# First layer of a two-layer encoder: another order of loads, norms, low halves and roots, four PSUM banks for the first tiles

## The reference, cut to what matters

```python
x = layer_norm(x, ln0_g, ln0_b)
for i in range(2):
    h = x @ w_in[i]                                  # 1024 -> 1536 columns
    qa, ka, va, qb, kb, vb = split(h)                # 512 | 128 | 128 | 512 | 128 | 128
    oa = softmax(rope2d(rms(qa)) @ rope2d(rms(ka)).T) @ va      # all keys
    ob = window_softmax_with_sink(rope1d(qb) @ rope1d(kb).T) @ vb
    mix = concat(rms(oa), rms(ob)) @ w_out[i]
    x = layer_norm(ALPHA * x + mix)
    gate = sigmoid(x @ w_ple_gate[i] + b)
    x = layer_norm(ALPHA * x + conv_glu(x) + gate * (p[i] @ w_ple[i]))
```

## Time and profile before

| | us |
|---|---|
| median of three runs | 1205.07 |
| the profiled execution | 1204.98 |
| its span (first to last instruction) | 1203.0 |
| TensorE busy | 1186.2 (99%) |
| VectorE, ScalarE, GpSimd busy | 524.5, 483.5, 585.3 |
| first matmul of the products | 15.97 |
| first scores | 70.25 |
| last matmul | 1195.08 |

### The profile page before, as it was taken

The page is one execution under the profiler, slowest core; times in us unless marked ns, Lnnn a source line. Parts: engine busy times, 40 slices in busy tenths (PEclk is TensorE's granted clock), DMA queues, the critical chain, the costliest instruction groups (busy, mean ns, idle before and its releaser), DMA issues.

```text
span 1203.0 us, 16482 instructions
## 1 busy us (share of the span) xinstructions
PE 1186.2 (99%) x5784; PEld 971.0 (81%) x5784; DVE 524.5 (44%) x1094; ACT 483.5 (40%) x890; POOL 585.3 (49%) x338
## 2 busy tenths in 40 slices
PE   7999999999999999999999999999999999999997
PEld 6787778888888888888888777788888888888886
DVE  7777857522121234211587788374221122431107
ACT  3457763244343333323144777433443343332310
POOL 6565754455444444343254756634554443434330
PEclk9999999999999999999999999999999999999999
DMA  6321213344333332223132202333433333322301
GB/s 223 87 71 54 89 53 106 122 125 138 97 95 87 105 106 88 88 92 104 54 80 79 73 34 71 140 105 88 140 106 103 99 93 96 97 74 102 105 35 70
DMA packets 121753, 113.45 MB, mean 94 GB/s; under 512 B 6752, under 2 KB 97888, under 8 KB 121696
## 3 DMA queue, kind: packets, MB, share of 16 engines
q1 hardware_dynamic: 121696, 112.71, 30.1%
HBM read 110.60 MB, written 2.10 MB: 94 GB/s over the span
## 4 chain that ended last, share of the span: by engine, by line
PE 95%; DVE 1%; POOL 1%; DVEq 1%; DMA 1%; issue 0%; SPq 0%
PE ps L1238 29%; PE ps L1240 28%; PE ps L1239 28%; PE ps L1404 3%; PE ps L1390 3%; PE ps L1378 1%; PE ps L1380 1%; PE ps L1248 1%; PE ps L1361 1%; POOL w_lo L544 1%; DMA x<-in_x_prompt_dram 1%; POOL ln_r L540 0%; DVEq L886 0%; DVEq L932 0%; PE ps L1415 0%
## 5 line engine op out<-in xcount | busy, mean ns | idle before, releaser
L534 POOL TENSOR_TENSOR w_lo<-raw,w_hi 128x1024 fp32r<-128x1024 f32 x188 | 453.1, 2412 | 404.6 <-ACT w_hi L645 404.5
L1238 PE MATMUL ps<-xt_hi,w_hi 128*128 128x512 f32 x704 | 273.9, 389 | 0.0
L1239 PE MATMUL ps<-xt_lo,w_hi 128*128 128x512 f32 x704 | 273.9, 389 | 0.0
L1240 PE MATMUL ps<-xt_hi,w_lo 128*128 128x512 f32 x704 | 273.9, 389 | 0.0
L645 ACT ACTIVATE w_hi<-raw 128x1024 fp32r<-128x1024 f32 x188 | 197.8, 1055 | 132.2 <-PE ps L1240 61.4
L1238 PE MATMUL ps<-w_hi,stat 128*128 128x512 f32 x480 | 187.8, 391 | 0.0
L1239 PE MATMUL ps<-w_lo,stat 128*128 128x512 f32 x480 | 187.1, 390 | 0.0
L1240 PE MATMUL ps<-w_hi,stat 128*128 128x512 f32 x480 | 187.1, 390 | 0.0
L1238 PEld LDWEIGHTS ps<-xt_hi,w_hi 128*128 128x128 f32 x704 | 132.2, 188 | 27.5
L1239 PEld LDWEIGHTS ps<-xt_lo,w_hi 128*128 128x128 f32 x704 | 132.2, 188 | 27.4
L1240 PEld LDWEIGHTS ps<-xt_hi,w_lo 128*128 128x128 f32 x704 | 132.2, 188 | 27.3
(11 more groups left out here) (123 smaller groups left out, 1323.7 us busy)
## 6 DMA issues: line engine op xcount, KB each, us to landing
raw<-in_w_up_dram SPq DMA_DIRECT2D x88, 512.0 KB, 3.8
raw<-in_w_down_dram SPq DMA_DIRECT2D x44, 512.0 KB, 3.2
raw<-in_w_in_dram SPq DMA_DIRECT2D x22, 512.0 KB, 3.7
raw<-in_w_out_dram SPq DMA_DIRECT2D x16, 512.0 KB, 3.3
raw<-in_w_ple_gate_dram SPq DMA_DIRECT2D x16, 512.0 KB, 3.3
scratch<-in_ln_g_dram SPq DMA_DIRECT2D x5, 512.0 KB, 4.1
scratch<-in_ln_b_dram SPq DMA_DIRECT2D x5, 512.0 KB, 6.0
raw<-in_w_ple_dram SPq DMA_DIRECT2D x4, 512.0 KB, 3.3
```

What stands on the lines that cost most here:

```text
L534: pool.tensor_tensor(w_lo[:, n, :], raw[:, n % RAW, :], w_hi[:, n, :].bitcast(F32), ALU.subtract).then_inc(w_split.sem, 1)
L1238: pe.matmul(out, a[0], b[0], start=first, stop=False)
L1239: pe.matmul(out, a[0], b[1], start=False, stop=False)
L1240: return pe.matmul(out, a[1], b[0], start=False, stop=last)
```

## The change

In the first layer alone, and before it:

- **Loads.** SyncE's order becomes tile 0 of x, slot 0, gain, shift, slot 1, tile 1, slot 2, tile 2, slot 3, tile 3. Before it was tile 0, gain, shift, tile 1, slots 0, 1, 2, tile 2, slot 3, tile 3.
- **GpSimd.** Root 0, low halves 0, 1, root 1, low halves 2, 3, root 2, low halves 4, 5, root 3, low halves 6, 7; then the roots of the rotations of c = 0 without low halves between them. c = 1 is as before.
- **VectorE.** The statistics of tile t + 1 and then `norm_lo(t)` follow the scaling of tile t. `norm_lo(3)` now stands before `gain_tables`, so both it and the tables stand before `rotate(0, 0)`. `qkt_lo` of n - 2 precedes `rotate` n (before: `qkt_lo` of n - 1 followed it).
- **TensorE.** The first product starts before tile 1 is transposed, in a new form, `first_quarter`: hi by hi, then the products with `xt_lo`, then those with `w_lo`, each group with its own wait. Tile 1 is transposed after the third quarter; `norm_in` 2 and 3 stand in the middle of products 1 and 2. Turned tiles 0 to 5 are transposed behind product 3, in the middle of 4, in the middle of and behind 5, behind 6, and in the middle of 7 (before: in the middle of 2, behind 2, 3, 4, 5, 6). `keep_warm` is 8, 4 and 3 rounds (before 8 and 9), the last inside the first quarter.
- **ScalarE.** `first_hi(3)` before tile 1's copies; `body_hi(7)` is moved forward to n = 2; the copies of turned tiles move with TensorE's steps. For n = 4 to 7 `body_hi(4 + n)` still comes first of all.

In both layers the products use the banks 0, 1, 6, 7 in turn (for c = 2: 0 and 1), so that product n waits for the rotation of n - 4 (c = 0, 1 and the first two of c = 2), and the squares go to `late` in place of `scratch`, without the wait for the four norms. `pv` 0 and 1, which write banks 6 and 7, wait for the rotations of n = 6 and 7.

```diff
-WARM = (8, 9)
+WARM = (8, 4, 3)
+WIN_BANK = (0, 1, 6, 7, 0, 1, 6, 7, 0, 1, 0, 1)
@@ pe_plan(layer)
+        if layer == 0:
+            within = {1: [("norm_in", 2)], 2: [("norm_in", 3)], 4: [("rot", 0, 1)], 5: [("rot", 0, 2)], 7: [("rot", 1, 1)]}
+            behind = {3: [("rot", 0, 0)], 5: [("rot", 0, 3)], 6: [("rot", 1, 0)]}
@@ sync
             load_x(0)
             first_load(0)
+            sp.dma_start(ln_g, bcast(ln0_g)).then_inc(first_gain_landed.sem, 16)
+            sp.dma_start(ln_b, bcast(ln0_b)).then_inc(norm_landed.sem, 16)
             first_load(1)
+            load_x(1)
             first_load(2)
@@ gpsimd
             ln_root(0, 1)
-            ln_root(1, 2)
             first_lo(0)
             first_lo(1)
-            ln_root(2, 3)
+            ln_root(1, 2)
             first_lo(2)
             first_lo(3)
-            ln_root(3, 4)
+            ln_root(2, 3)
...
+                if layer == 0:
+                    body_lo(4)
+                    body_lo(5)
+                    ln_root(3, 4)
+                    body_lo(6)
+                    body_lo(7)
@@ scalar, for n in 0..7
-                        body_hi(4 + n)
-                        if n == 2:
+                        if layer or n != 3:
+                            body_hi(4 + n)
+                        if layer == 0 and n in (1, 2):
+                            norm_hi(n + 1, tr_full.at(layer, TR["norm_in", n + 1] + 1))
+                        if layer == 0 and n == 2:
+                            body_hi(7)
+                        if layer == 0 and n in (4, 5, 7):
+                            qkt_evac(*divmod({4: 1, 5: 2, 7: 5}[n], TT))
+                        if layer and n == 2:
                             qkt_evac(0, 0)
                         win(c, t)
-                        if n < 2:
+                        if layer == 0 and n in (3, 5, 6, 7):
+                            qkt_evac(*divmod({3: 0, 5: 3, 6: 4, 7: 6}[n], TT))
@@ vector
+            first_stats(0)
             for t in range(TT):
...
                 norm_scale(t, t + 1, centred)
-                if t in (1, 2):
-                    norm_lo(t - 1, 2 * t - 1)
+                if t < TT - 1:
+                    first_stats(t + 1)
+                    norm_lo(t, 2 * t + 1)
+            norm_lo(TT - 1, 2 * TT - 1)
             def gain_tables(landed):
@@ vector, for n in 0..7
-                        if n == 2:
-                            qkt_lo(0, 0)
+                        if n == 2 or (layer == 0 and n > 2):
+                            qkt_lo(*divmod(n - 2, TT))
                         if n == 2 * TT - 1:
                             maxima(0)
                         rotate(c, t)
@@ tensor
+                def first_quarter(q):
+                    w = slot(q)
+                    at = [xt(2 * q + k, 0) for k in range(2)]
+                    out = ps[:, WIN_BANK[0], :]
+                    pe.wait_ge(w_hi_done.sem, q + 1)
+                    pe.wait_ge(xt_hi_done.sem, q // 2 + 1)
+                    for k in range(2):
+                        pe.matmul(out, at[k][0], w[0][:, k, :], start=(q == 0 and k == 0), stop=False)
+                    if q == 0:
+                        keep_warm(WARM[2])
+                    pe.wait_ge(xt_split.sem, q // 2 + 1)
+                    for k in range(2):
+                        pe.matmul(out, at[k][1], w[0][:, k, :], start=False, stop=False)
+                    split(q)
+                    for k in range(2):
+                        ins = pe.matmul(out, at[k][0], w[1][:, k, :], start=False, stop=(q == 3 and k == 1))
+                    return ins
```

More of the change, by code:

```diff
@@ L65, with pe_plan @@
 assert STREAM % SLOTS == 0 and LOOPED % 4 == 0
-def pe_plan():
+def pe_plan(layer):
     steps = []
@@ L142, in encoder @@
             w_out, ln1_g, ln1_b, w_up, w_down, ln2_g, ln2_b, w_ple, w_ple_gate, b_ple_gate, rope, y_prompt, y_sample):
-    STEPS = pe_plan()
-    TR, TR_LAYER = transposes_of(STEPS)
+    STEPS = [pe_plan(layer) for layer in range(DEPTH)]
+    TR, TR_LAYER = transposes_of(STEPS[0])
+    assert transposes_of(STEPS[1]) == (TR, TR_LAYER)
     TR_BEFORE = 4
@@ L178, in encoder @@
         turned = scratch[:, 0, :]
-        squares = scratch[:, 2:4, :]
+        squares = late[:, 0:2, :]
         ln_g = scratch[:, 0:2, :].rearrange("p a n -> p (a n)")
@@ L586, in _ @@
                         w = (HEADS, KV)[c]
-                        if c == 0:
+                        if c == 0 and layer:
                             body_lo(4 + n)
@@ L677, in win @@
                     n = c * TT + t
-                    bank = ps[:, n % 2, :]
+                    bank = ps[:, WIN_BANK[n], :]
                     wait_win(act, layer, c, t)
                     if c == 0:
-                        act.wait_ge(ln_done.sem, ln_done.at(layer, 0))
                         if n >= 2:
@@ L1130, in glu @@
                     dve.tensor_tensor(dst, dst, ps[:, bank + 1, :], ALU.mult).then_inc(h_done.sem, 1)
-                norm_lo(2, xt_hi_done.at(layer, 1))
+                if layer:
+                    norm_lo(2, xt_hi_done.at(layer, 1))
                 for c in range(2):
@@ L1141, in _ @@
                         rotate(c, t)
-                        if n == 0:
+                        if n == 0 and layer:
                             norm_lo(3, xt_hi_done.at(layer, 3))
-                        if n >= 2:
+                        if n == 2 * TT - 1 or (layer and n >= 2):
                             qkt_lo(*divmod(n - 1, TT))
@@ L1261, in keep_warm @@
                     for _ in range(8):
-                        pe.matmul(ps[:, 0, 0:P], ident_b[:, :], mask[:, :], start=True, stop=True)
+                        pe.matmul(ps[:, WIN_BANK[1], 0:P], ident_b[:, :], mask[:, :], start=True, stop=True)
             pe.wait_ge(const_made.sem, 1)
             keep_warm(WARM[0])
[L1266 to L1271, removed]
+            for b in norm_t(0, 1):
+                pass
+            keep_warm(WARM[1])
             for layer in range(DEPTH):
@@ L1312, in win_quarter @@
                             pe.wait_ge(xt_split.sem, 16 * layer + 2 * t + 2)
-                        if n >= 2:
-                            pe.wait_ge(rot_done.sem, rot_done.at(layer, n - 1))
+                        if n >= 4:
+                            pe.wait_ge(rot_done.sem, rot_done.at(layer, n - 3 if n < 10 else n - 1))
                         else:
@@ L1340, in signal @@
                         ins.then_inc(full.sem, 1)
-                for step in STEPS:
+                for step in STEPS[layer]:
                     kind = step[0]
@@ L1346, in _ @@
                         for q in (2 * half, 2 * half + 1):
-                            ins = win_quarter(c, t, q)
+                            if (layer, c, t) == (0, 0, 0):
+                                ins = first_quarter(q)
+                            else:
+                                ins = win_quarter(c, t, q)
                             signal(ins, win_full, q == 3, t)
+                            if (layer, c, t, q) == (0, 0, 0, 2):
+                                for b in norm_t(1, 2):
+                                    pe.wait_ge(xt_split.sem, b + 1)
                     elif kind == "win_part":
```

34 lines of the change are left out of this document (16 added, 18 removed).

## The result

The changed kernel takes 1209.66 us (median of 6 runs, 1209.05 to 1210.54), the kernel before 1205.12 (6 runs, 1204.66 to 1205.71): ratio 1.0037, 95% interval 1.0027 to 1.0048. It is 0.4% slower, above the predicted range of 1203.6 to 1208.6. Its profiled execution took 1209.17 us with a span of 1207.4 (before 1204.98 and 1203.0), so 4.2 us more in time and 4.4 in span.

The account below looks back on a forecast made before the run. TensorE, busy 99% of the span, was taken to bound the kernel. First scores moving from 70.3 to 71.3 gave +1.0 us: 1206.0 for the profiled execution, 1206.1 for the median; range 1203.6 to 1208.6.

Parts of the forecast that it names:

- The chain to the scores: From VectorE's rotation 4 through GpSimd, slot 10's load, ScalarE and VectorE: first scores at 71.3, TensorE idle 4.3 us before them.
- the clock's fall: Rival: TensorE's clock falls in the 4.3 us gap before the first scores, costing 2.2 us, to 1208.3; chance 0.27.
- VectorE's pace: Rotations of c = 0 at 3.05 us and low halves at 1.35, without idle time from 39.3: rotation 4 begins at 55.5.
- Loads and tile 0: Start: gain lands at 7.4, low half 0 holds centring 0 until 10.2; scaling ends at 11.4, 2.2 us later than before.
- First products: TensorE: product 1 starts at 23.7, product 4 at 42.8, 4.1 us ahead, 3.2 in work.
- Tables: VectorE: table products, 1.4 us alone, meet low half 7 and end at 39.3, so rotation 0 begins 7.9 us later.
- The walk: Following each engine's list to the first scores: 70.3 before (70.25 in the trace), 71.3 after.
- The links from there: After rotation 4: low half 8 to 59.2, slot 10 landed at 63.1, copy to 65.5, first scores at 71.3.
- The gain reaches the scores: Rival: VectorE keeps up, first scores at 67.0, time 1201.8; needs rotation 4 at 51.2, below a floor of 54.9; chance 0.1.
- The ends of the unknowns: Slot load time -0.6 to +0.6, centring not held -1.1, first loads later +1.0: together -1.0 to +2.8, 1204.1 to 1207.9.

Follow-up runs that it names:

- Kernel 6: The changed kernel with the first loads in the order of before (tile 0, gain, shift, tile 1, slots 0 and 1): 1208.33 us, ratio to before 1.0031.
- Kernels 3: The changed kernel with ScalarE's copy of turned tile 4 ahead of slot 10's high half, slot 11's behind tile 7's squares: 1205.82 us, 1.0007.
- 4: The changed kernel, ScalarE's order as changed, with GpSimd's low halves of slots 8 and 9 ahead of the roots of tiles 4 and 5: 1206.15 us, 1.0004.
- kernel 1: The changed kernel with 64 warm-up matmuls on TensorE between product 7 and the first scores of layer 0: 1207.49 us, 1.0022.
- Kernel 9: The kernel before with four banks and only the change's later transposes, copies and splits of turned tiles: 1213.75 us, 1.0075.
- kernels 7: The kernel before with four banks for the first eight products and the waits that go with them, nothing else: 1203.28 us, 0.9986.
- 8: The kernel before with four banks and 24 warm-up matmuls ahead of the wait for the low half of slot 2: 1203.22 us, 0.9984.
- 11: The kernel before with four banks, `first_quarter`, two warm-up rounds in its third quarter, turned tile 0 transposed behind product 2, tile 1 in mid product 3: 1202.21 us, 0.9979.
- kernel 10: The kernel before with four banks, turned tile 0 transposed behind product 2 and tile 1 in the middle of product 3: 1203.74 us, 0.9987.
- kernel 2: The changed kernel with twelve in place of eight first rounds of warm-up matmuls: 1209.52 us, 1.0037.

## Why the prediction was wrong

The chain to the scores was right. The time came out of the range because of two terms of the sum: the clock's fall, put at nothing in the likeliest case (2.2 us), and VectorE's pace, 1.15 us short. Either alone would have left the time within 1208.6 (1208.3 and 1207.3); together they did not.

- **Loads and tile 0.** Right: centring 0 took 2.12 us (8.06 to 10.2, forecast end 10.2), held by low half 0, though gain landed at 8.0 and not 7.4. Kernel 6 puts the whole order of loads at some 0.6 us at the scores.
- **First products.** Nearly right: the waits of the earlier trace rows are gone, but product 1 starts at 24.22 (forecast 23.7) and product 4 at 43.49 (42.8), behind a wait of 0.4 for rotation 0 that the forecast did not have. TensorE was through with product 7 at 68.0, not 67.0. That the gap came out near its forecast (4.45 against 4.3) is luck in part: both of its ends were late, by 1.0 and 1.15 us.
- **Tables.** Right: a table product of 2.48 us, rotation 0 at 39.52 (39.3).
- **VectorE's pace.** This term was too small. The walk took 3.05 us for a rotation of c = 0 and 1.35 for a low half, 4.4 per tile; the rotations came at 42.94, 47.45, 52.10 and 56.76, 4.65 us for each of the last two, and rotation 0 had a wait of 0.50 in it (whose releaser the profile does not show) and took 3.42. With 0.2 from its start, rotation 4 began at 56.76, not 55.5. Both readings were short. The low half's own row shows 1.39, and the next operation starts 1.42 behind it in the change. The rotation read is one of the quicker ones in the trace of before; a later one takes 3.23 there to its low half (47.38 to 50.61), as rotations 2 and 3 do in the change.
- **The links from there.** All right to 0.15 us as durations, and all 1.1 to 1.2 late: low half 8 ended at 60.43 (59.2), slot 10 landed at 64.2 (63.1), copies to 66.65 (65.5), scores at 72.45 (71.3). Kernels 3 and 4, which cut it at two places with the same gain, show that it is one chain.
- **The clock.** This is the failed step, with the pace beside it: the clock's fall was a rival at 0.27, and its 2.2 us stood in no term of the sum. The prediction had it decide "from a gap of about 3.3 us on", taken from the single fall after the last matmul, and held against it that the gap of 2.3 us before kept 1.00. The forecast gap of 4.3 us lay beyond 3.3: the working itself asked for the fall as the likeliest case. The trace has it 2.5 us behind the end of product 7 (68.0 to 70.5), and behind gaps of 2.1 us in kernels 3 and 4, so 3.3 was no lower bound. The cost forecast for it, 2.2 us, stands against the 1.9 to 2.2 of kernel 1. With the clock in the sum the forecast would have been 1208.3, and with the pace 1209.5, against 1209.66.
- **What ends the other side.** "The gain reaches the scores" was ruled out by the late transposes of the turned tiles. Kernel 9 shows that they cost even more on their own, and kernels 7, 8 and 11 that the banks' release is a gain where they are not deferred. If the banks were worth in the change what they are worth in kernel 8, its +4.5 would be banks -1.9, clock +1.9 (kernel 1) and +4.5 for the other order; no run has the change with the old banks, so this split is an estimate.
- **Two sums.** 1204.98 - 3.3 is 1201.7, not 1201.8. The ends of the unknowns as listed add up, with the 1.0, to -0.7 and +2.6, not to -1.0 and +2.8. Neither changes the outcome.

Open stays how kernel 11's gain over kernel 8 (0.5 us by the medians, 0.8 at the first scores) divides between the early quarters and the transposes' places.

## What to carry to other kernels

Where the engine that bounds the kernel gains on the others, follow the others to the next point where it needs them: here TensorE's gain of the first products came back as a wait of 4.5 us, behind a high half queued ahead of a copy. Price a gap on TensorE with the fall of its clock as the likely case, and look whether a few matmuls into a free bank can fill it. When the pitch of a repeated step decides, read it from one start to the next, over several repeats, and not from a single one.

## What the runs showed of the hardware

- The granted clock fell to 1.2 GHz behind shorter gaps than the one the prediction had gone by: after 1.97 us at 10 us in the change, after 2.06 and 2.09 us at 70 us in kernels 3 and 4, 2.16 us at 22 us in kernel 10. The gap's length did not decide alone: the kernel before kept 1.00 behind a wait of 2.15 us at 20 us, and kernel 10 behind one of 2.02 us at 10 us. In kernel 3 the fall came only at about 70.7 (0.72 from 70.5 to 71.0), with TensorE at work again since 70.07. Even one kernel has both kinds of runs: kernel 7 has ten from 1202.86 to 1203.58 and one at 1205.33, and that one shows the fall. With 24 matmuls in the gap all 11 runs lay within 0.9 us.
- At the lower clock the change's matmuls stood 0.43 us apart (74.72 and 75.15 us) where they stand 0.23 apart at the full one (67.38 and 67.61), and the fall at 70 us cost 1.9 to 2.2 us of the end time. The one at 12 us cost nothing that can be measured (kernel 2).
- VectorE and GpSimd hold each other up, both ways. A centring beside a low half took 2.12 us (1.28 alone) and a table product 2.48 (0.28 alone); and GpSimd's root beside a centring 1.54 us, 0.56 alone.
